# Rows of the merged activations stored by row tile, the router's choice made per row tile, and the gather in three parts

## The reference

```python
merged = gates[..., :d] * (ha @ w_up_a[l]) + gates[..., d:] * (hb @ w_up_b[l])
h = h + merged @ w_out[l]
u = rms_norm(h, norm_ffn_g[l])
group_logits = uf @ w_rg + b_rg                       # 4 groups
g_idx = jnp.argmax(group_logits, axis=-1)
exp_logits = (uf @ w_re + b_re).reshape(n, 4, 8)      # 8 experts in each group
sel = jnp.take_along_axis(exp_logits, g_idx[:, None, None], axis=1)[:, 0]
top_v, top_i = lax.top_k(sel, 2)
gates = p_group * jax.nn.softmax(top_v, axis=-1)
# each row goes through its 2 experts: (silu(x @ w_gate_e) * (x @ w_up_e)) @ w_down_e
```

## Time and profile before

| what | value |
|---|---|
| median of 3 runs | 886.07 us (886.01 to 886.84) |
| the profiled execution | 886.23 us, span 884.5 us |
| PE busy | 836.7 us, 95% |
| DVE, ACT, POOL busy | 342.2, 273.0, 82.1 us |
| granted TensorE clock, mean | 0.986 |
| bytes moved | 253.85 MB, mean 287 GB/s |

### The profile page before, as it was taken

The page is one execution under the profiler, slowest core; times in us unless marked ns, Lnnn a source line. Parts: engine busy times, 40 slices in busy tenths (PEclk is TensorE's granted clock), DMA queues, the critical chain, the costliest instruction groups (busy, mean ns, idle before and its releaser), DMA issues.

```text
span 884.5 us, 10432 instructions
## 1 busy us (share of the span) xinstructions
PE 836.7 (95%) x4321; PEld 527.9 (60%) x4321; DVE 342.2 (39%) x479; ACT 273.0 (31%) x401; POOL 82.1 (9%) x64
## 2 busy tenths in 40 slices
PE   5999999999999999999999999888998898999996
PEld 4888888788888887536535354352352352533685
DVE  6899549962651616511020120101100101015865
ACT  7666346733332226202010100101001001002777
POOL 3436380000000000000000000000000000001000
PEclk9999999999999999999999999999899999999999
DMA  9222222211525764899999999999999999998902
GB/s 260 97 93 96 95 96 96 96 49 49 189 96 207 296 257 179 349 423 425 401 428 426 428 426 429 426 428 428 428 428 428 426 425 430 427 421 347 356 2 95
DMA packets 45334, 253.85 MB, mean 287 GB/s; under 512 B 8868, under 2 KB 9960, under 8 KB 31976
## 3 DMA queue, kind: packets, MB, share of 16 engines
q1 hardware_dynamic: 42696, 248.21, 69.2%
q0 software_dynamic: 2304, 4.20, 1.2%
q10 hardware_dynamic: 288, 0.79, 0.2%
HBM read 246.89 MB, written 10.49 MB: 291 GB/s over the span
## 4 chain that ended last, share of the span: by engine, by line
PE 44%; DMA 14%; issue 1%; DVE 1%; ACT 1%; DVEq 0%; ACTq 0%
PE bank L1459 42%; DMA ring<-in_w_down_e_dram 11%; DMA ring<-in_w_gate_e_dram 3%; PE bank L1689 1%; PE bank L1785 0%; ACT L1046 0%; ACT r_rounded L901 0%; PE bank L1529 0%; DVE pick L1250 0%; DVE r_rounded L439 0%; ACT r L999 0%; ACT L999 0%; ACT junk L887 0%; PE bank L1775 0%; ACT gain L895 0%
## 5 line engine op out<-in xcount | busy, mean ns | idle before, releaser
L1459 PE MATMUL bank<-ring_rounded,ring_rounded 128*128 128x512 f32 (+1 forms) x696 | 245.0, 389 | 0.3 <-DVE ring_rounded L1134 0.3
L1459 PE MATMUL bank<-r_rounded,ring_rounded 128*128 128x512 f32 (+1 forms) x744 | 234.4, 389 | 0.7 <-DVE ring_rounded L1081 0.6
L1459 PEld LDWEIGHTS bank<-r_rounded,ring_rounded 128*128 128x128 f32 x744 | 138.9, 188 | 30.4 <-DVE ring_rounded L1081 0.9
L1459 PEld LDWEIGHTS bank<-ring_rounded,ring_rounded 128*128 128x128 f32 x696 | 130.3, 188 | 28.1 <-issue 1.3
L1459 PE MATMUL bank<-ring,gain 128*64 128x512 f32 x472 | 118.0, 604 | 9.3 <-issue 8.1
L1459 PE MATMUL bank<-ring,hT 128*64 128x512 f32 x400 | 112.3, 624 | 6.7 <-DMA ring<-in_w_down_e_dram 6.7
L1459 PE MATMUL bank<-ring,junk 128*64 128x512 f32 x472 | 115.5, 592 | 0.0
L1459 PEld LDWEIGHTS bank<-ring,gain 128*64 128x64 f32 x472 | 36.1, 138 | 76.3 <-issue 73.5
L1459 PEld LDWEIGHTS bank<-ring,junk 128*64 128x64 f32 x472 | 37.6, 137 | 71.4 <-issue 71.3
L730 POOL DMA_INDIRECT expert_rows<-r,row_i x16 | 16.5, 1032 | 669.3 <-DVE r L1346 669.3
L945 ACT ACTIVATE r<-bank,factor 128x512 f32<-128x512 f32 x16 | 11.0, 687 | 215.2 <-PE bank L1459 215.2
(11 more groups left out here) (226 smaller groups left out, 761.6 us busy)
## 6 DMA issues: line engine op xcount, KB each, us to landing
ring<-in_w_up_e_dram SPq DMA_DIRECT2D x29, 2048.0 KB, 29.6
ring<-in_w_gate_e_dram SPq DMA_DIRECT2D x24, 2048.0 KB, 27.9
ring<-in_w_down_e_dram SPq DMA_DIRECT2D x22, 2048.0 KB, 32.0
ring<-in_w_in_dram SPq DMA_DIRECT2D x18, 1024.0 KB, 7.3
r<-in_w_gate_e_dram SPq DMA_DIRECT2D x5, 2048.0 KB, 27.9
r<-in_w_down_e_dram SPq DMA_DIRECT2D x4, 2048.0 KB, 34.2
ring<-in_w_down_e_dram SPq DMA_DIRECT2D x7, 1024.0 KB, 21.6
ring<-in_w_up_e_dram SPq DMA_DIRECT2D x6, 1024.0 KB, 11.0
```

Of the source, the lines that this page charges most:

```text
L1459: return nc.tensor.matmul(*a, **k)
```

## The change

- `merged`, its high and its low part are stored by row tile: the earlier trace rows[column tile][128 rows]. A quarter of a slot is then free when one row tile of the last block is done.
- The refill of slots 5 to 8: 5 and 6 (`OF_WEIGHTS`) as before; 7 and 8 (`OF_MERGED`) get their first two quarters when tile 5 is done, the third when tile 6 is done, the last when tile 7 is done.
- `route(i)` works on one row tile, with VectorE's max (the eight largest of a row, in order) and max_index (where they stand). The four group logits get four columns of padding (`GW` = 8, filled on POOL), so that eight are there to choose from. It stands on VectorE before residual(c), for i = c - 5; route(3) behind the last tile.
- `rows_split` moves from VectorE to POOL, all four of them.
- In tiles 5 to 7 the transposes stand before product 6 (counted from 0), scores before 9, logits before 13, all inside the tile; places(0), of row tiles 0 and 1, follows the transposes of tile 7.
- ScalarE copies the transposed halves first, then takes the norm, copies the scores and rounds the rows.
- Places, picks and the gather are in three parts: row tiles 0 and 1, row tile 2, row tile 3. The `keep_busy` products go; parts of the first gather stand between the router steps of row tile 3.

```diff
@@ -158,8 +163,8 @@
         ha_low = r2_r[:, :].rearrange("p (c t) -> p c t", c=NX)
         hb_high = r4_r[:, :].rearrange("p (g t) -> p g t", g=NB)[:, :, PAD:W]
         hb_low = slot_r[6][:, SLOT - NB * S:SLOT].rearrange("p (g t) -> p g t", g=NB)
-        merged_high = slot_r[5][:, :].rearrange("p (k t) -> p k t", k=KD)
-        merged_low = r3_r[:, :].rearrange("p (k t) -> p k t", k=KD)
+        merged_high = slot_r[5][:, :].rearrange("p (i k t) -> p k i t", i=TT, k=KD)
+        merged_low = r3_r[:, :].rearrange("p (i k t) -> p k i t", i=TT, k=KD)
         def block_half(slot, h):
             return slot.rearrange("p (k f) -> p k f", k=KD)[:, 4 * h:4 * h + 4, :]
...
@@ -397,7 +411,9 @@
         PIECES = {LEAD: 3, LEAD + 1: 3, LEAD + 2: 2, LEAD + 3: 2}
         LEFT_LAST = range(5, LEAD)
-        PIECES.update({n: 2 for n in LEFT_LAST})
+        OF_WEIGHTS, OF_MERGED = LEFT_LAST[:2], LEFT_LAST[2:]
+        PIECES.update({n: 2 for n in OF_WEIGHTS})
+        PIECES.update({n: 3 for n in OF_MERGED})
         def landed(n):
...
@@ -432,11 +448,13 @@
                                                      op0=ALU.mult, op1=ALU.subtract)
             ins.then_inc(pg_low_ready, 1)
-        def rows_split(dve, i):
-            dve.wait_ge(rows_high_ready, i + 1)
-            dve.wait_ge(rows_psum, 2 * i)
-            nc.vector.tensor_tensor(rows_low(i), h1_by_k(i), rows_high(i), ALU.subtract).then_inc(rows_low_ready, 1)
+        def rows_split(pool, i):
+            pool.wait_ge(rows_high_ready, i + 1)
+            if i >= 1:
+                pool.wait_ge(rows_psum, 2 * i)
+                pool.wait_ge(rows_low_ready, i)
+            nc.gpsimd.tensor_tensor(rows_low(i), h1_by_k(i), rows_high(i), ALU.subtract).then_inc(rows_low_ready, 1)
         def lows_at(n, h):
...
@@ -557,12 +575,21 @@
             for n in range(1, LEFT_LAST.start):
                 sp.wait_ge(tile_done, 4 * (FIRST_OUT if n < 3 else FIRST_OUT + 1))
                 load_expert(n)
+            sp.wait_ge(tile_done, 4 * len(blocks) - 2)
+            for n in OF_MERGED:
+                load_part(n, 0, 2, slot_full[n])
+            sp.wait_ge(tile_done, 4 * len(blocks) - 1)
+            for n in OF_MERGED:
+                load_part(n, 2, 3, slot_full[n])
             sp.wait_ge(first_half_used, 1)
-            for n in LEFT_LAST:
+            for n in OF_WEIGHTS:
                 load_part(n, 0, 2, slot_full[n])
             sp.wait_ge(tile_done, 4 * len(blocks))
-            for n in LEFT_LAST:
+            for n in OF_WEIGHTS:
                 load_part(n, 2, 4, slot_full[n])
+            for n in OF_MERGED:
+                load_part(n, 3, 4, slot_full[n])
             sp.wait_ge(rounds_ready, 1)
             wg = w_ple_gate[0].rearrange("(p k) n -> p k n", p=P)
...
@@ -711,6 +741,8 @@
                                         ALU.subtract).then_inc(pooled, 1)
                 pool.wait_ge(pooled, g + 1)
             low(5)
+            for i in range(TT):
+                rows_split(pool, i)
             pool.wait_ge(rounds_ready, 1)
...
@@ -904,21 +936,14 @@
                 act.wait_ge(scores_psum, i + 1)
                 nc.scalar.activation(scoresT(i), bank[0][0:64 + NL, i * P:(i + 1) * P], ACT.Copy).then_inc(scores_ready, 1)
-            for i in range(TT - 1):
+            for i in range(TT):
+                copy_row_half(i, 0)
+                if i < TT - 1:
+                    copy_row_half(i, 1)
                 act.wait_ge(h1_ready, TT + i + 1)
                 row_norm(i)
-                if i > 0:
...
-                    row_high(i)
                 copy_scores(i)
-            copy_row_half(TT - 1, 0)
-            act.wait_ge(h1_ready, 2 * TT)
-            row_norm(TT - 1)
-            copy_scores(TT - 1)
-            row_high(TT - 1)
+                row_high(i)
             act.wait_ge(gdiff_ready, 1)
...
@@ -1203,42 +1228,30 @@
             def bc(ap, n):
                 return ap.unsqueeze(2).to_broadcast([P, ap.shape[1], n])
-            def first_max(scores, n, best, index, cands, onehot):
...
-                dve.wait_ge(routed_ready, 2 * half + 2)
+            def route(i):
+                dve.wait_ge(logits_psum, i + 1)
+                after(v.scalar_tensor_tensor(out=lg[:, i, :], in0=bank[LOGITS_BANK[i]][:, i * 64:i * 64 + NL],
+                                             scalar=rstd[:, TT + i:TT + i + 1], in1=brt[:, :], op0=ALU.mult, op1=ALU.add))
+                after(v.max(out=group_top[:, i, :], in_=lg[:, i, 0:GW]))
+                after(v.max_index(out=group_at[:, i, :], in_max=group_top[:, i, :], in_values=lg[:, i, 0:GW]))
+                after(v.tensor_tensor(g4[:, 1, i, :], iota[:, 0:NG], group_at[:, i, 0:1].to_broadcast([P, NG]), ALU.not_equal))
+                after(v.scalar_tensor_tensor(out=el[:, i, :].rearrange("p (g e) -> p g e", g=NG),
+                                             in0=g4[:, 1, i, :].unsqueeze(2).to_broadcast([P, NG, PG]), scalar=-2 * BIG,
+                                             in1=lg[:, i, GW:NL].rearrange("p (g e) -> p g e", g=NG), op0=ALU.mult, op1=ALU.add))
+                after(v.max(out=expert_top[:, i, :], in_=el[:, i, :]))
+                after(v.max_index(out=expert_at[:, i, :], in_max=expert_top[:, i, :], in_values=el[:, i, :]))
+                after(v.tensor_tensor(chosen[:, :, i, :], iota[:, 0:NE].unsqueeze(1).to_broadcast([P, 2, NE]),
+                                      expert_at[:, i, 0:2].unsqueeze(2).to_broadcast([P, 2, NE]), ALU.is_equal))
+                v.tensor_tensor(routed_bf[:, i, :], oh1[:, i, :], oh2[:, i, :], ALU.add).then_inc(routed_ready, 1)
+                v.tensor_tensor(routed[:, i, :], oh1[:, i, :], oh2[:, i, :], ALU.add).then_inc(routed_ready, 1)
+            def find_places(group):
+                at = slice(row_groups[group][0], row_groups[group][-1] + 1)
+                dve.wait_ge(places_psum, group + 1)
+                dve.wait_ge(routed_ready, 2 * at.stop)
                 after(v.scalar_tensor_tensor(out=cand[:, at, :],
-                                             in0=bank[2][:, 2 * half * NE:2 * (half + 1) * NE].rearrange("p (i e) -> p i e", i=2),
+                                             in0=bank[2][:, at.start * NE:at.stop * NE].rearrange("p (i e) -> p i e", e=NE),
                                              scalar=1.0, in1=routed[:, at, :], op0=ALU.add, op1=ALU.mult))
                 after(v.tensor_scalar(place[:, 0:NE, at].rearrange("p e i -> p i e"), cand[:, at, :], -1.0, None, ALU.add))
...
@@ -1280,31 +1293,32 @@
                 if ("ua", 0) == (kind, c):
                     dve.wait_ge(lru_in, 16 * 11)
+                    dve.wait_ge(pads_ready, 1)
                     v.tensor_tensor(wrt[:, :, :], wrt[:, :, :], gain_col[:, :].unsqueeze(2).to_broadcast([P, KD, NL]),
                                     ALU.mult).then_inc(wrt_ready, 1)
-                if ("out", c) == (kind, 2 * TT - 1):
-                    route(0)
                 if kind == "out":
-                    if TT < c < 2 * TT - 1:
-                        rows_split(dve, c - TT - 1)
+                    if c == TT + 1:
+                        dve.wait_ge(pads_ready, 2)
+                    if c > TT:
+                        row_rstd(c - TT - 1)
+                        route(c - TT - 1)
                     residual(c)
...
                         v.memset(bank[0][32:64, :], 0.0).then_inc(scores_cleared, 1)
-                    if c > TT:
-                        row_rstd(c - TT - 1)
-            find_places(0)
+                    if c == 2 * TT - 2:
+                        find_places(0)
+            find_places(1)
             dve.wait_ge(rows_psum, 2 * TT)
...
                           bank[4 + (2 * TT - 1) % 3][:, :].rearrange("p (k t) -> p k t", k=4)).then_inc(last_rows_ready, 1)
-            rows_split(dve, TT - 2)
             row_rstd(TT - 1)
-            route(1)
-            v.tensor_tensor(g4[:, 0, :, :], lg[:, :, 0:NG], bc(t4[:, 0, :], NG), ALU.subtract).then_inc(gdiff_ready, 1)
-            v.tensor_tensor(t4[:, 6, :], t4[:, 4, :], t4[:, 2, :], ALU.subtract).then_inc(ediff_ready, 1)
-            find_places(1)
-            rows_split(dve, TT - 1)
+            route(TT - 1)
+            v.tensor_tensor(g4[:, 0, :, :], lg[:, :, 0:NG], group_top[:, :, 0:1].to_broadcast([P, TT, NG]),
+                            ALU.subtract).then_inc(gdiff_ready, 1)
+            v.tensor_tensor(t4[:, 6, :], expert_top[:, :, 1], expert_top[:, :, 0], ALU.subtract).then_inc(ediff_ready, 1)
+            find_places(2)
             after(v.tensor_reduce(t4[:, 0, 0:1], bank[2][:, 4 * NE:5 * NE], AX.X, ALU.max))
             v.tensor_scalar(rounds_i[:, :], t4[:, 0, 0:1], 1.0 / C, 0.5 - 0.5 / C, ALU.mult, ALU.add).then_inc(rounds_ready, 1)
...
             of_u, of_hb, of_merged = ((by_k(uT_high), by_k(uT_low)), (by_k(hb_high), by_k(hb_low)),
                                       (by_k(merged_high), by_k(merged_low)))
+            def routing_of(i, product):
```

(60 more changed lines are left out.)

91 lines of the change are left out of this document (34 added, 57 removed).

## The result

The changed kernel takes 892.34 us (median of 4 runs, 891.64 to 895.0) against 886.05: a ratio of 1.0072, 95% interval 1.0057 to 1.0086. It is 6.3 us slower; 893.6 was forecast. The profiled execution is the longest of the four, 895.0 us with a span of 893.3, 8.8 us over the span before.

A forecast was written before the change was run, and what follows sets the result against it. The start of the expert loop was taken to set the whole rest, transfers bounding late in the span. Waits less savings, +7.15 us, plus 0.4 for the clock gave +7.5 on 886.07: 893.6 us, range 882.8 to 899.

The forecast's parts named there:

- What bounds: Late in the span: the expert loop's start sets the whole rest, shifting every refill one for one.
- Refilling in pieces: Slots 7 and 8, last block: 7.4 us of transfer moved before 342.80, by itself worth nothing.
- The choice: VectorE's router choice per row tile: about 2.2 us to routed_bf, about 2.8 less than before.
- The moved split: rows_split on POOL: VectorE's comparison and sums wait for POOL's end in each row tile; shift 4D−5.65, +7.15 us.
- D: Duration of one rows_split on POOL: taken as 3.2 us, between 2.3 and 4.2.
- The stride: POOL's strided split read: the skill's added half would make D 3.46 us and the shift +8.2.
- The clock: TensorE's clock falling behind new stalls: about 2 us if at the last gather, 0.4 us as mean.
- rarer case: Lock plus half clock in tiles 6 and 7 and at the loop's start: 898 to 900 us, chance 0.14.
- the waits less the savings: Four VectorE waits on POOL up to the gather's end, savings on choice and gather included: +7.15 us.
- The rival without the lock: POOL's read does not hold VectorE's choice, tiles run without stall: −3.1 us, 883; chance 0.17.
- The gather in three parts: Before the expert loop: only row tile 3 depends on the last places; 1.4 us less.

The follow-up runs named there:

- e6: e1_vector with slots 5 to 8 refilled at the old two moments, without the early pieces: 883.83 us, ratio 0.996.
- e5: Kernel before the change plus only merged rows stored by row tile and early piecewise refill of slots 7 and 8: 886.46 us, ratio 0.9999.
- e1_vector: Changed kernel with all four rows_split instructions back on VectorE: 883.15 us, ratio 0.9966.
- e3: Changed kernel with each POOL split replaced by three zero fills that write SBUF and read none; low parts not computed: 881.85 us, ratio 0.9954.
- e4: Changed kernel with POOL's splits reading both inputs in flat order, without a stride (low parts wrong): 889.41 us, ratio 1.0032.
- e8: Changed kernel with useless filler products in TensorE's two waits behind tile 7: 890.29 us, ratio 1.0043.
- e9: e2 with the split of row tile 3 free again to start on POOL behind row_high: 885.89 us, ratio 0.9992.
- e2: Changed kernel with the same four POOL splits, each held back until its row tile's choice is over or pick made: 883.42 us, ratio 0.9965.

## Why the prediction was right

- **What bounds.** The start of the loop shifts the span one for one, within 0.3 us in ten of eleven kernels. The exception, e6, is the one in which the stream was made the later of the two.
- **Refilling in pieces.** Worth nothing by itself: shown by e5. "Without it a loop that starts more than about a microsecond earlier would be held back by the stream": the span is 1.2 us longer at a loop 3.2 us earlier (e6), and by the medians it is 0.7. The direction was right, the price small.
- **The choice.** Forecast 2.2 us from the scaled logits to the end of routed_bf; in e1_vector, where nothing holds it, it runs from 353.02 to 355.19, 2.17 us. MAX8 takes 0.17 to 0.20, the two instructions of max_index about 0.25 together. The comparison starts 1.72 us behind the scaled logits (forecast 1.8); POOL started 1.15 to 1.52 behind them in the changed kernel (forecast 1.25). So it won each time, by 0.2 us and more.
- **The moved split.** D was taken as 3.2 and is 2.98 (2.88 to 3.04). The waits are where they were placed: all four on the comparison, and behind it the residual and the transposes in row tiles 0 and 1, the places product in row tiles 2 and 3. Forecast starts of the transposes, with D = 2.98: 336.1, 346.1 and 356.6; measured 335.57, 345.25 and 356.12, the last with 0.8 us of low clock in it. The rule that I cited from the Trainium skill, "SBUF — State Buffer", section "Who interferes with whom", has a finer point: a VectorE instruction with two SBUF inputs contends with a GpSimd instruction that reads SBUF, not with one that only writes it. The traces agree: the comparison takes 2.50 to 2.90 us beside a split and 0.22 or 0.23 beside fills (e3). The scaling from SBUF to SBUF is held by both, by the split in the earlier trace rows and by the fills in e3.
- **The stride.** By the Trainium skill's "GPSIMD Engine Reference", section "Performance pitfalls for Q7 kernels", the strided read should cost half as much again; e4 shows 2.37 flat and 2.98 with one of two inputs strided, a quarter more. My own 3.2 was nearer.
- **The clock.** Forecast as 0.4 us in the mean, with half clock as a rarer case of 0.14. Measured: 2 to 2.5 us (e8), and the gather behind the last wait was long in the profiled executions of the changed kernel (6.68), of e9 (5.56) and of e4 (5.58). This is one of two terms that were mis-sized. In tiles 6 and 7, where the rarer case had it fall too, the clock stayed at 1.00 behind waits of 1.74 and 1.49 us.
- **What offset it.** The other is +7.15 for the waits less the savings. At D = 2.98 the forecast's sum gives 4×2.98−5.65 = +6.3 (from its terms, 357.7 less 363.38, the 5.65 should be 5.68). e8, at full clock, shows 3.8 by its median and +4.1 by the start of its loop: its transposes start at 335.25, 344.93 and 354.98 and its loop at 367.43, against 336.1, 346.1, 356.6 and 369.6. Of these last 2.2 us, 0.4 were there at the transposes of row tile 0 (324.46 against 324.85). Behind POOL's end each of the four steps is 0.3 us shorter than I had it, and in front of POOL's start 0.1 to 0.2. In tile 5 the two sums are the main part: they take 0.21 us (334.30 to 334.51), where I had 0.5. So the mechanism was right, but that 893.6 lies as near as 1.3 us to the measured time is in part luck: one term was about 3 us too large, the other about 2 too small. The first expert product, forecast near 370.5, comes at 371.85, in a trace with 4.1 us of low clock.
- **The rival without the lock.** Its price, −3.1 us or 883, is what the kernels without the waits measured: 883.15 (e1) and 883.42 (e2), with the first expert product at 360.16 and 360.63 where the rival had the gather end at 360.25.
- **The gather in three parts.** About 2 us of TensorE between the last places and the start of row tile 3, as forecast: the 32 products behind the last places follow without a wait in e3, 4.08 us. From the end of routed_bf to the loop it takes 5.83 us in the kernel before, 4.97 in e1 and 4.29 in e3. So the forecast saving of 1.4 us comes in full only where the low part of row tile 3 does not hold the gather up (1.5 in e3, 0.9 in e1).

## What to carry to other kernels

Work moved to an engine that is idle is not free if it holds up a neighbour: look in the trace for a short VectorE instruction that ends when a POOL instruction ends, and price a POOL read by what VectorE has behind it at that moment. Here its start mattered more than its length; the same four instructions made the kernel 8.9 us slower at one moment than a little later, where they cost nothing measurable against the splits on VectorE (883.42 against 883.15). A wait in front of TensorE should be priced with the clock that may fall behind it.

## What the runs showed of the hardware that I had not expected

- A POOL fill (memset) of 0.95 us left the VectorE comparison with two SBUF inputs at 0.23 us, but held a scaling of 32 elements for 0.4 to 0.6 us, to the end of the fill.
- A wait of TensorE of 2.87 us was followed by a granted clock of 0.50 from 365 to 371 us and a gather 1.6 times as long, and one of 2.02 us by 0.50 from 355 to 357; behind waits of 1.74, 1.49 and, in e4_flat, 1.40 it stayed at 1.00, and so it did behind the gap of 3.29 in the earlier trace rows, so the length of a wait alone does not tell. With small products without use in the two waits behind tile 7 it stayed at 1.00 there too.
- POOL's split of 1024 elements takes 2.37 us flat and 2.98 with one input strided by 32 bytes; on VectorE the same split takes 2.11 us against an estimated 1.15 flat, half of the 2.29 for 2048 elements. The estimate is a little low: a VectorE comparison of 1024 elements takes 1.22 in e1_vector, which would make the factor 1.7 instead of the 1.84 of the forecast.
